# Latent attention: exponentials and rotation products in PSUM, the layer's residual on GpSimd and ScalarE, one tile a pair of heads

## What is computed

```python
def mla_mixer(h, positions, ...):
    q_c, kv_c, k_r, z = split(h @ w_in)
    q_c, kv_c = rms_norm_2(q_c, q_norm_g), rms_norm_2(kv_c, kv_norm_g)
    q_nope, q_rope = split(einsum('bsr,rhd->bshd', q_c, w_uq))
    q_rope, k_rope = apply_rope(q_rope, cos, sin), apply_rope(k_r, cos, sin)
    q_lat = einsum('bshd,rhd->bshr', q_nope, w_uk)
    # per block i of 128 queries and per head, keys in chunks of 64:
    s = (q_lat . kv_c + q_rope . k_rope) * ATTN_SCALE
    p = softmax(where(mask, s, -inf))
    o_lat = p . kv_c
    return (einsum('bshr,rhd->bshd', o_lat, w_uv) * silu(z)) @ w_out

x = layer_norm(DEEPNORM_ALPHA * x + (1.0 + gate) * mla_mixer(x * (1 + scale) + shift), ln_g, ln_b)
```

## Time and profile before

| | |
|---|---|
| median of 3 runs | 2105.71 us (2102.74 to 2109.05) |
| profiled execution | 2105.03 us |
| its span on the core | 2103.0 us |
| mean granted TensorE clock | 0.971 of full speed |
| busy | TensorE 94%, weight load 78%, VectorE 48%, ScalarE 40%, GpSimd 38% |
| latent attention's place in the span | 1676 to 1984 us |

### The profile page before, as it was taken

The page is one execution under the profiler, slowest core; times in us unless marked ns, Lnnn a source line. Parts: engine busy times, 40 slices in busy tenths (PEclk is TensorE's granted clock), DMA queues, the critical chain, the costliest instruction groups (busy, mean ns, idle before and its releaser), DMA issues.

```text
span 2103.0 us, 29110 instructions
## 1 busy us (share of the span) xinstructions
PE 1975.6 (94%) x9640; PEld 1638.0 (78%) x9640; DVE 1016.6 (48%) x2286; ACT 840.0 (40%) x1520; POOL 805.9 (38%) x382
## 2 busy tenths in 40 slices
PE   7999999999988999999999997999999789999896
PEld 5897888888777889878888886777887567777684
DVE  5555665211636666356553116658113655555414
ACT  4564222233444666342222325222222465555432
POOL 3533544444363100135444443445443332232340
PEclk9999999999999989999999999999999999999998
DMA  7532544222242112135442322323232111121121
GB/s 240 159 103 101 195 166 167 93 97 100 71 150 66 47 46 76 36 114 190 160 159 100 100 92 72 107 91 105 90 100 80 60 53 59 50 70 40 61 80 40
DMA packets 70026, 209.55 MB, mean 100 GB/s; under 512 B 9739, under 2 KB 15115, under 8 KB 69948
## 3 DMA queue, kind: packets, MB, share of 16 engines
q1 hardware_dynamic: 57724, 174.72, 25.2%
q10 hardware_dynamic: 12224, 33.85, 5.0%
HBM read 196.90 MB, written 8.49 MB: 98 GB/s over the span
## 4 chain that ended last, share of the span: by engine, by line
PE 58%; issue 21%; POOL 9%; DVE 8%; ACT 4%; POOLq 0%; DVEq 0%; ACTq 0%
PE bank L949 14%; PE bank L951 14%; PE bank L950 14%; POOL wsp L445 9%; PE bank L1227 3%; PE bank L1382 2%; DVE gen L2037 2%; PE bank L1200 1%; PE bank L1401 1%; PE bank L1211 1%; PE bank L1095 1%; PE bank L1393 1%; ACT wsp L531 1%; PE bank L1072 1%; PE bank L1223 1%
## 5 line engine op out<-in xcount | busy, mean ns | idle before, releaser
L445 POOL TENSOR_TENSOR wsp<-raw,wsp 128x1024 fp32r<-128x1024 f32 x294 | 730.5, 2491 | 1051.4 <-ACT wsp L531 1051.3
L949 PE MATMUL bank<-xs,wsp 128*128 128x512 f32 x1320 | 522.1, 396 | 19.5 <-issue 8.4
L950 PE MATMUL bank<-xs,wsp 128*128 128x512 f32 x1320 | 516.1, 391 | 0.0
L951 PE MATMUL bank<-xs,wsp 128*128 128x512 f32 x1320 | 516.1, 391 | 0.0
L531 ACT ACTIVATE wsp<-raw 128x1024 fp32r<-128x1024 f32 x294 | 306.9, 1052 | 229.9 <-PE bank L951 199.9
L949 PEld LDWEIGHTS bank<-xs,wsp 128*128 128x128 f32 x1320 | 249.4, 189 | 76.8 <-issue 15.3
L949 PE MATMUL bank<-xk,wsp 128*128 128x512 f32 x752 | 295.3, 393 | 9.4 <-DVE xk L1503 5.1
L950 PE MATMUL bank<-xk,wsp 128*128 128x512 f32 x752 | 294.2, 391 | 0.0
L951 PE MATMUL bank<-xk,wsp 128*128 128x512 f32 x752 | 294.2, 391 | 0.0
L951 PEld LDWEIGHTS bank<-xs,wsp 128*128 128x128 f32 x1320 | 249.2, 189 | 52.5
L950 PEld LDWEIGHTS bank<-xs,wsp 128*128 128x128 f32 x1320 | 249.6, 189 | 52.0 <-issue 1.4
(11 more groups left out here) (286 smaller groups left out, 2504.2 us busy)
## 6 DMA issues: line engine op xcount, KB each, us to landing
raw<-weights SPq DMA_DIRECT2D x294, 512.0 KB, 3.5
gen<-ada ACTq DMA_DIRECT2D x48, 512.0 KB, 3.5
tmp<-mid SPq DMA_DIRECT2D x64, 128.0 KB, 3.0
bias_b<-bias_row ACTq DMA_DIRECT2D x1, 4096.0 KB, 38.1
mid<-bias_b SPq DMA_DIRECT2D x8, 512.0 KB, 3.9
hT<-xT SPq DMA_DIRECT2D x2, 1024.0 KB, 10.1
bias_a<-bias_row ACTq DMA_DIRECT2D x1, 2048.0 KB, 18.0
mid<-bias_a SPq DMA_DIRECT2D x8, 256.0 KB, 2.9
```

The costliest lines, as they stand in the source:

```text
L445: pool.tensor_tensor(wsp[:, slot, 1, :], raw[:, slot, :], wsp[:, slot, 0, :].bitcast(F32), ALU.subtract).then_inc(w_ready, 1)
L949: pe.matmul(dst, w[0], x[0], start=first, stop=False)
L950: pe.matmul(dst, w[0], x[1], start=False, stop=False)
L951: return pe.matmul(dst, w[1], x[0], start=False, stop=last)
```

## The change

- The exponential is written over the scores in their PSUM bank. The multiplication by the reciprocal sum reads it there and writes `o_p`. The scores of step m wait for the multiplication of step m-2, no longer for its exponential. The wait for the transposes of step m-2 moves from ahead of the exponential on ScalarE to ahead of the multiplication on VectorE.
- In `rotate` the sine product is written over bank 3, and the additions read it there. For the keys the sine product and the sum lie in bank 7.
- VectorE's `residual(1)` and ScalarE's `residual_bias(1)` ahead of the pairs are taken out. GpSimd multiplies one tile of hT by `rstd` in each pair, behind the first split; ScalarE scales it and adds the bias at the end of the pair.

```diff
@@ -509,12 +509,19 @@
                 split_lo(u % RING, u)
                 if u == O_H + 4:
                     rope_lo(0)
+            def residual(j):
+
+                pool.tensor_tensor(hT[:, j, :], hT[:, j, :], rstd[:, :], ALU.mult).then_inc(mod_x, 1)
+
             with pool.Fori(0, PAIRS - 1) as hp:
                 for k in range(RING):
                     u = O_H + 5 + k
                     split_lo(u % RING, hp * RING + u)
+                    if k == 0:
+                        residual(hp)
                     if k == 2:
                         rope_lo(hp + 1)
+            residual(PAIRS - 1)
             for u in range(O_H + 5 + RING * (PAIRS - 1), UNITS):
                 split_lo(u % RING, u)
 
@@ -872,11 +879,10 @@
             def o_exp_of(m, r, hp):
 
                 b, w = m % 2, P * (m % 4 + 1)
-                if m >= 2:
-                    act.wait_ge(o_t, hp * 8 + (8 * r + m - 1))
+                scores = bank[SCORE_BANKS[r][b]][:, 0:w]
                 act.wait_ge(o_nm, hp * 8 + (8 * r + m + 1))
-                act.activation(o_p[b][:, 0:w], bank[SCORE_BANKS[r][b]][:, 0:w], ACT.Exp, scale=QK_SCALE,
-                               bias=stat[:, b, 1:2], accum_out=stat[:, b, 2:3]).then_inc(o_exp, 1)
+                act.activation(scores, scores, ACT.Exp, scale=QK_SCALE, bias=stat[:, b, 1:2],
+                               accum_out=stat[:, b, 2:3]).then_inc(o_exp, 1)
 
             def o_turn(m, r, hp):
                 b, w = m % 2, P * (m % 4 + 1)
@@ -915,18 +921,21 @@
                     keep_latent(r + 1, hp)
                     rope_hi(r + 1, hp)
                     split_hi(u0 + 6, hp)
+                j = hp + r
+                act.wait_ge(mod_x, j + (16 + DC + 1))
+                act.activation(hT[:, j, :], hT[:, j, :], ACT.Identity, scale=modg[:, 1, bass.ds(j + 16, 1)],
+                               bias=modg[:, 1, bass.ds(j + 24, 1)]).then_inc(alpha_done, 1)
 
             act.wait_ge(kr_ready, 2)
             act.wait_ge(consts, 12)
             for h in range(2):
-                act.activation(krs[h][0:HD, :], r_raw[0], ACT.Copy).then_inc(kr_ready, 1)
+                act.activation(krs[h][0:HD, :], bank[7][0:HD, :], ACT.Copy).then_inc(kr_ready, 1)
             nope_hi(0, 0)
             split_hi(O_C + 8)
             act.wait_ge(kvt_mm, 1)
             act.activation(kvt, bank[6][:, :], ACT.Copy).then_inc(kvt_ready, 1)
             keep_latent(0, 0)
             rope_hi(0, 0)
-            residual_bias(1)
             with act.Fori(0, PAIRS - 2, 2) as hp:
                 for r in range(2):
                     pair_of_heads(r, hp, False)
@@ -1371,7 +1380,7 @@
                 b, e, blk = m % 2, m // 4, m % 4
                 dst = bank[SCORE_BANKS[r][b]]
                 if m >= 2:
-                    pe.wait_ge(o_exp, hp * 8 + (8 * r + m - 1))
+                    pe.wait_ge(o_prob, hp * 8 + (8 * r + m - 1))
                 else:
                     pe.wait_ge(mid_ready, hp * 2 + (2 * r + MID_O - 1 + m))
                 if blk == 0:
@@ -1999,12 +2008,13 @@
 
             dve.wait_ge(trig_ready, 2)
             dve.wait_ge(unit_used, O_C + 4)
+            keys = bank[7][0:HD, :]
             step(dve.tensor_tensor(tmp[0:HD, 2, :], bank[3][0:HD, :], cosb[0:HD, :], ALU.mult))
-            dve.tensor_tensor(tmp[0:HD, 3, :], bank[3][HD:P, :], sinb[HD:P, :], ALU.mult).then_inc(kr_ready, 1)
+            dve.tensor_tensor(keys, bank[3][HD:P, :], sinb[HD:P, :], ALU.mult).then_inc(kr_ready, 1)
             dve.wait_ge(kr_ready, 1)
-            dve.tensor_tensor(r_raw[0], tmp[0:HD, 2, :], tmp[0:HD, 3, :], ALU.add).then_inc(kr_ready, 1)
+            dve.tensor_tensor(keys, tmp[0:HD, 2, :], keys, ALU.add).then_inc(kr_ready, 1)
             dve.wait_ge(kr_ready, 4)
-            dve.tensor_tensor(krs[0][HD:P, :], r_raw[0], krs[0][0:HD, :].bitcast(F32), ALU.subtract).then_inc(kr_ready, 1)
+            dve.tensor_tensor(krs[0][HD:P, :], keys, krs[0][0:HD, :].bitcast(F32), ALU.subtract).then_inc(kr_ready, 1)
 
             def nope_lo(r, hp):
                 for e in range(2):
@@ -2016,11 +2026,11 @@
 
                 dve.wait_ge(unit_used, hp * RING + (O_H + 1 + RING * r))
                 dve.tensor_tensor(tmp[:, 0, :], bank[2][:, :], cosb, ALU.mult).then_inc(r_part, 1)
-                dve.tensor_tensor(tmp[:, 1, :], bank[3][:, :], sinb, ALU.mult).then_inc(r_part, 1)
+                dve.tensor_tensor(bank[3][:, :], bank[3][:, :], sinb, ALU.mult).then_inc(r_part, 1)
                 dve.wait_ge(r_part, hp * 4 + (4 * r + 2))
                 for e in range(2):
                     half = slice(e * HD, e * HD + HD)
-                    dve.tensor_tensor(r_raw[e], tmp[half, 0, :], tmp[half, 1, :], ALU.add).then_inc(r_part, 1)
+                    dve.tensor_tensor(r_raw[e], tmp[half, 0, :], bank[3][half, :], ALU.add).then_inc(r_part, 1)
 
             def o_max_of(m, r, hp):
                 b, w = m % 2, P * (m % 4 + 1)
@@ -2034,7 +2044,10 @@
                 dve.wait_ge(o_exp, hp * 8 + (8 * r + m + 1))
                 dve.reciprocal(stat[:, b, 3:4], stat[:, b, 2:3]).then_inc(o_rec, 1)
                 dve.wait_ge(o_rec, hp * 8 + (8 * r + m + 1))
-                dve.tensor_scalar(o_p[b][:, 0:w], o_p[b][:, 0:w], stat[:, b, 3:4], None, ALU.mult).then_inc(o_prob, 1)
+                if m >= 2:
+                    dve.wait_ge(o_t, hp * 8 + (8 * r + m - 1))
+                dve.tensor_scalar(o_p[b][:, 0:w], bank[SCORE_BANKS[r][b]][:, 0:w], stat[:, b, 3:4], None, ALU.mult
+                                  ).then_inc(o_prob, 1)
 
             def latent_lo(e, r, hp):
                 dve.wait_ge(ol_hi, hp * 2 + (2 * r + e + 1))
@@ -2066,7 +2079,6 @@
 
             nope_lo(0, 0)
             rotate(0, 0)
-            residual(1)
             with dve.Fori(0, PAIRS - 2, 2) as hp:
                 for r in range(2):
                     pair_of_heads(r, hp, False)
```

## The result

| | before | changed |
|---|---|---|
| median | 2105.3 us (4 runs, 2102.74 to 2109.05) | 2073.47 us (4 runs, 2071.57 to 2074.32) |
| ratio | 1 | 0.9846, 95% interval 0.9829 to 0.9863 |
| span of the profiled execution | 2103.0 us | 2069.5 us |
| mean granted clock in it | 0.971 | 0.978 |

32 us faster. The changed kernel's lines move: the multiplication is L2049, the exponential L884, the transposes L1402, the residual's two instructions L514 (GpSimd) and L926 (ScalarE).

The account below looks back on a forecast made before the run. TensorE, busy 94%, bounds the kernel, so time comes from its gaps or clock. 22.4 (seven pairs) + 7.5 (pair 0) + 1.7 (keys) = 31.6 us off 2105.0 gives 2073.4, by median 2074; range 2064 to 2087.

Parts of the forecast that it names:

- The stall: Latent attention: SBUF multiplication L2037 stands still 4.39 us until GpSimd's three splits end; reading PSUM removes it, 2.47 us gained.
- three rows: L2037 and L2005, inputs in SBUF, ended with GpSimd's runs; L2018, one input in PSUM, took 0.68 us beside a split.
- The destination: Rival: writing SBUF is what makes L2037 wait for GpSimd, so the stall stays; 2115 us, chance 0.04.
- the exponential slowed by writing its own bank: Rival: PSUM read and write take turns, 34 us over 64 exponentials; 2108 us, chance 0.04.
- The price of the product: Multiplication reading PSUM costs 0.74 us on 512 columns, down to 0.34 on 128; growth 0.63 us a head.
- The chain late next: With the stall gone, the softmax chain (maximum to normalised product) is what TensorE waits for next in each pair.
- T(0) to T(3): From the transposes of step 0 to those of step 3, a pair's first head: 7.43 us before, 6.3 forecast.
- T(3) to T(7): From the transposes of step 3 to those of step 7, second head: 7.97 us becomes 8.4, 0.4 lost.
- The residual: Residual moved from ahead of pair 0 into the pairs: TensorE's 5.90 us gap closes, pair 0 gives 7.5 us, cost 0.
- off the path: The rotation's sine product in bank 3 was taken to lie off the path, with no gain counted for it.
- Writes into PSUM: VectorE and ScalarE writing PSUM taken as no change; 0.03 us either way per exponential, 2 us in all.
- the sum: Gains of 22.4 us in seven pairs, 7.5 in pair 0 and 1.7 from the keys: 31.6 us.

Follow-up runs that it names:

- PSUM alone: Kernel before with only the exponential and its product moved to PSUM; residual, keys and rotation as before: 2077.93 us, ratio 0.9872.
- a reordering: Exponentials in SBUF with the wait on GpSimd, plus TensorE issuing scores of step m ahead of transposes of step m-2: 2063.6 us against 2067.51 without, same chip.
- The SBUF kernel with the wait: Changed kernel with exponential and product back in SBUF, GpSimd's later splits held until the pair's eight multiplications are done: 2068.37 us, on another chip 2067.51, ratio 0.9829 both.

## Why the prediction was right

**The stall.** That the product L2037 stood still for GpSimd, and only because its input lay in SBUF, was read from three rows; undoing the PSUM part brings it back, and holding GpSimd back removes it without PSUM. One of the three was weaker than I took it for: L2018 starts 0.03 us ahead of the split that it was set against. Its neighbour L2019, which also reads PSUM, starts inside that split and takes the same time. VectorE before:

```profile
1680.83 0.68 DVE L2019 TENSOR_TENSOR tmp<-bank,gen 128x512 f32<-128x512 f32 x1
...
1695.16 1.93 DVE L2037 TENSOR_SCALAR gen<-gen,stat 128x128 f32<-128x128 f32 x1
```

The destination, which stayed in SBUF, doesn't matter: that rival is out by the 0.351 us of L2049, as is the exponential slowed by writing its own bank (0.340 and 0.662 us). The Trainium skill, "SBUF — State Buffer", section "Who interferes with whom", states an exclusive lock on a pair of ports between the two engines, for VectorE instructions in a two-port mode or with two SBUF inputs; the runs agree in that such an instruction stands still altogether and one that reads PSUM doesn't. How long it stands still varies: to the end of GpSimd's back-to-back run in pairs 1 to 7 of the kernel before (4.39 to 4.41 us), but only to the end of one split in its pair 0 (1.93 us, above) and in pairs 2 and 4 with exponentials back in SBUF (1.98 us), with GpSimd's next instruction following at once. What decides between the two isn't known.

**The price of the product.** 0.74, 0.61, 0.48 and 0.34 us forecast as the middle of two rows; 0.751, 0.617, 0.484 and 0.351 measured. The growth by the cycles of the Trainium skill's page "VectorE: DVE Perf Modes", 0.92 us a head, was too much; 0.65 was measured.

**The chain late next.** T(0) to T(3): 6.3 forecast, 6.34 in pair 0; pair 1 has 6.59. There VectorE's product of step 2 starts 0.28 us later behind its reciprocal than in other pairs, in a kernel without GpSimd beside it too, and I haven't found why. T(3) to T(7): 8.4 forecast, 8.24 measured in pairs 0 and 1, 8.42 in the last. A pair gained 3.10 where I had 3.2. The new idle of TensorE sits at T(2) and T(7), as said.

**The residual.** The 5.9 us ahead of pair 0 came as forecast, but the prediction gave all of them to the residual, and that is wrong. From the start of the three splits to T(0) of pair 0 is 27.70 us before, 24.94 with keys and rotation in PSUM, 21.64 with the residual moved too (the run with exponentials back in SBUF), and 20.04 changed. With the keys' 1.75 apart, 1.0 is the rotation's, which the prediction had "off the path", 3.3 are the residual's, and 1.6 come from pair 0's own product, which took 1.93 us (above) and stands still no more. The gap was read rightly from the profile, and it closed; but that the residual's move alone would close it was wrong, and the total held because the two other parts of the change did the rest. In its new place the residual is free (34.53 us a pair without it, 34.55 with), but only there: where the stall stays, it puts 1.25 us more of GpSimd in front of a pair's first product, and moving it cost some 3 us. The parts don't add up: PSUM alone gives 27 us, the other two parts together about nothing without it, and 5 with it.

**Writes into PSUM.** Taken as no change; ScalarE's exponential became 0.026 us shorter at each width. The Trainium skill, "ScalarE: Activation LUTs", section "Step-by-step: what each stage is for", has PSUM as the faster destination; the trace agrees with that small number.

**What the sum didn't hold.** To T(7) of the last pair, the attention gained 30.9 us against 31.6 forecast. The spans differ by 33.5 because 0.9 came ahead of the stage and 1.7 behind it, in code that is the same. Of the 1.7 most is the clock near the end: the windows view has 42 matmuls in 14.7 us of TensorE at 0.97 and 0.86 before (2072 to 2092 us), and in 13.2 us at 1.00 changed (2040 to 2060). The profiled execution was also the fastest of the changed kernel's four. That the median landed within 1 us is partly such luck; the terms are what holds.

## To carry to other kernels

A VectorE instruction that takes ten times its usual time, and ends when an instruction or a run of them on GpSimd ends, isn't slow: it stands still. One on SBUF alone was freed here by reading PSUM, and also by having GpSimd begin its run later, where GpSimd had the time. Try the second first: here two waits gave what the whole rewrite gave, kept the cheaper SBUF form, and left the score banks free early enough for a reordering that took another 4 us. Before work is moved to an engine, look at what that engine already holds up.

## What the runs showed of the hardware that was not expected

The same idle stretch doesn't always lower TensorE's clock. At the attention's end TensorE waits for the last values. The SBUF kernel with the wait was run twice, the same program on two chips; windows view of 20 us behind T(7), the second run first, then the first:

```profile
1939.74:1949.74 10.00, 5.96 (x28) 4.44 (x29) 4.08 (x6) 7.21 (x11) 7.69 (x4) 0.80 0.45 145
1949.74:1959.74 10.00, 10.00 (x39) 8.12 (x38) 0.69 (x1) 1.58 (x2) 3.55 (x2) 0.86 0.20 68
```

```profile
1944.00:1954.00 10.00, 5.85 (x32) 4.60 (x33) 4.14 (x6) 7.22 (x11) 8.11 (x4) 1.00 0.43 142
1954.00:1964.00 10.00, 10.00 (x46) 8.29 (x45) 0.69 (x1) 2.03 (x3) 3.71 (x2) 1.00 0.25 86
```

TensorE is busy 5.96 and 5.85 of the first 10 us, and one run has a mean granted clock of 0.80 and 0.86, the other 1.00, with 46 matmuls and not 39 in the second window. From T(7) to the end the two take 124.4 and 122.1 us. The changed kernel has 0.80 and 0.86 too and takes 124.4; the kernel before, whose clock also fell near the end, took 126.1. So 2 to 4 us of a comparison can come from whether the clock falls in such a stretch, outside the code that was changed, and even between two runs of one program. What decides whether it falls isn't shown.
